# Preparing each GLA chunk one block ahead, with doubled tiles, in a hybrid decoder layer

## What is computed

```
log_a = log_sigmoid(g_lr @ gla_w_gate + gla_b_gate) / 16
b = cumsum(log_a, within a chunk);  b_last = b at the chunk's end
q_dec = q * dk**-0.5 * exp(b);  k_inv = k * exp(-b);  k_end = k * exp(b_last - b)
a_intra = tril(q_dec @ k_inv.T)
o = a_intra @ v + q_dec @ state
state = exp(b_last) * state + k_end.T @ v
o_gla = head_rms_norm(o) * gla_norm_g * silu(g_r)
```

## Time and profile before

| what | value |
|---|---|
| time, median of 2 runs | 3582.77 us (3580.89 to 3584.64) |
| the profiled execution's own time | 3579.59 us |
| its span, core 6 (slowest of 3555.3 to 3577.9) | 3577.9 us |
| mean granted TensorE clock, core 6 | 0.805 |
| busy: PE, DVE, ACT, POOL | 61%, 44%, 43%, 10% |
| HBM over the span | 92 GB/s |

### The profile page before, as it was taken

One profiled execution on the slowest core, in us unless ns is written; L12 is line 12 of the kernel. 1 busy time (PEld: TensorE's weight loads), 2 busy tenths in 40 slices (PEclk: granted clock), 3 DMA queues, 4 the chain that ended last, 5 costly groups with the idle time before them and its releaser, 6 DMA issues.

```text
span 3577.9 us, 45263 instructions; the slowest of 8 cores (3555.3 to 3577.9 us)
## 1 busy us (share of the span) xinstructions
PE 2189.3 (61%) x12880; PEld 1112.3 (31%) x13060; DVE 1556.4 (44%) x3607; ACT 1539.4 (43%) x2278; POOL 357.7 (10%) x292
## 2 busy tenths in 40 slices
PE   4924541565756637677764667777546777775653
PEld 0313321343422224333322423333224333332221
DVE  0033231232443364555235555543465455334782
ACT  0000000062069911587662048877501788875130
POOL 1002113200000000122000002210000112000150
PEclk9856765755879968799887869999767899998787
DMA  9438763303300012111432311124321111333222
GB/s 198 149 118 123 125 130 109 126 1 103 104 1 1 1 70 90 52 50 42 124 112 94 101 36 50 52 71 129 103 78 57 60 42 36 101 107 128 77 70 74
DMA packets 208100, 294.80 MB, mean 82 GB/s; under 512 B 92386, under 2 KB 92531, under 8 KB 207219
## 3 DMA queue, kind: packets, MB, share of 16 engines
q1 hardware_dynamic: 127460, 248.34, 21.8%
q0 software_dynamic: 74064, 26.25, 6.1%
q10 hardware_dynamic: 6336, 17.30, 1.5%
HBM read 293.45 MB, written 34.11 MB: 92 GB/s over the span
## 4 chain that ended last, share of the span: by engine, by line
PE 37%; DMA 22%; DVE 15%; issue 12%; ACT 11%; POOL 2%; DVEq 1%; ACTq 0%; SPq 0%; POOLq 0%
PE PP L246 36%; ACT ARENA L252 10%; DMA ARENA<-wd_s 9%; DVE ARENA L255 5%; DVE ARENA L259 4%; DMA ARENA<-w_down 3%; DMA ARENA<-win_s 2%; DMA ARENA<-w_ada 2%; DVE ARENA L262 2%; DMA wu_s<-w_ff_up 2%; POOL ARENA L259 1%; DMA ARENA<-wout_s 1%; DVE ARENA L266 1%; DMA ARENA<-wg_s 1%; DMA ARENA<-w_out 1%
## 5 line engine op out<-in xcount | busy, mean ns | idle before, releaser
L246 PE MATMUL PP<-ARENA 128*128 128x512 bf16 (+3 forms) x4964 | 1003.0, 350 | 441.5 <-DMA ARENA<-wd_s 109.8
L252 ACT ACTIVATE ARENA<-PP 128x1024 f32<-128x1024 f32 (+3 forms) x1251 | 904.2, 744 | 567.5 <-PE PP L246 445.3
L246 PE MATMUL PP<-ARENA,KT 128*128 128x512 bf16 (+3 forms) x1869 | 609.4, 375 | 378.4 <-ACT ARENA L252 335.2
L252 ACT ACTIVATE ARENA<-ARENA 128x1024 bf16<-128x1024 f32 (+7 forms) x882 | 645.0, 733 | 409.4 <-DVE ARENA L725 147.1
L246 PEld LDWEIGHTS PP<-ARENA 128*128 128x128 bf16 (+2 forms) x5064 | 469.0, 102 | 875.0 <-issue 617.7
L255 DVE TENSOR_SCALAR STAT<-PP 128x4 f32<-128x4 f32 (+3 forms) x512 | 81.2, 159 | 744.8 <-PE PP L246 744.0
L259 POOL TENSOR_TENSOR ARENA<-ARENA 128x512 f32<-128x512 f32 (+1 forms) x198 | 271.9, 1373 | 1249.0 <-PE PP L246 409.5
L246 PEld LDWEIGHTS PP<-ARENA,KT 128*128 128x128 bf16 x1920 | 181.9, 103 | 673.5 <-issue 578.8
L246 PE MATMUL PP<-ARENA,NEGUB 128*128 128x512 bf16 (+3 forms) x947 | 355.9, 376 | 0.9
L252 ACT ACT_TABLE_LOAD x12 | 15.4, 1283 | 761.0 <-PE PP L246 755.7
L266 DVE COPY ARENA<-PP 128x512 f32<-128x512 f32 (+5 forms) x249 | 140.2, 564 | 346.5 <-PE PP L246 308.0
(11 more groups left out here) (65 smaller groups left out, 1269.6 us busy)
## 6 DMA issues: line engine op xcount, KB each, us to landing
ARENA<-wd_s SPq DMA_DIRECT2D x286, 256.0 KB, 2.7
ARENA<-wg_s SPq DMA_DIRECT2D x110, 256.0 KB, 2.6
ARENA<-win_s SPq DMA_DIRECT2D x50, 512.0 KB, 3.9
ARENA<-xw SPq DMA_DIRECT2D x49, 512.0 KB, 6.4
ARENA<-w_ada SPq DMA_DIRECT2D x12, 2048.0 KB, 12.6
ARENA<-wu_s SPq DMA_DIRECT2D x88, 256.0 KB, 2.6
ARENA<-win_s SPq DMA_DIRECT2D x78, 256.0 KB, 3.8
ARENA<-w_down ACTq DMA_DIRECT2D x22, 512.0 KB, 3.7
```

The lines of the kernel that those rows point to most:

```text
L246: return S.op("pe", lambda e: e.matmul(out, lhsT=lhsT, rhs=rhs, start=start, stop=stop), reads, writes)
L252: return S.op("act", lambda e: e.activation(out=out, in_=in_, func=func, bias=bias, scale=scale), reads, writes)
```

## The change

The body of phase B's loop is split into `X(j)`, the prep of block j, and `Y(j)`, all the rest. The calls are X(0), X(1), Y(0), X(2), Y(1), X(3), Y(2), Y(3) in each tile. `QD`, `KI`, `KE` and the decay columns get two buffers each, chosen by j % 2; `EU`, `LL`, `EB`, `ENB`, `ED` and all others keep one. Inside `Y` the state products, the update of `S2` and the cast to `S2B` now stand right behind the products `bo` and ahead of the copies `OC`; before, they stood behind the writes of `ON`. The list `deferred` is still served at the end of each block, now of `Y`.

```diff
--- before.py
+++ after.py
@@ -413,9 +413,9 @@
     EB = cv.take([P, 2, 128], F32)
     ENB = cv.take([P, 2, 128], F32)
     ED = cv.take([P, 256], F32)
-    QD = cv.take([P, 2, 128], BF16)
-    KI = cv.take([P, 2, 128], BF16)
-    KE = cv.take([P, 256], BF16)
+    QDs = [cv.take([P, 2, 128], BF16) for _ in range(2)]
+    KIs = [cv.take([P, 2, 128], BF16) for _ in range(2)]
+    KEs = [cv.take([P, 256], BF16) for _ in range(2)]
     AM = cv.take([P, 2, 2, 128], BF16)
     OC = cv.take([P, 2, 2, 128], F32)
     SQ = cv.take([P, 2, 2, 128], F32)
@@ -510,10 +510,12 @@
                 tm_job(21 + 2 * pi, qblocks, ev)
 
     def phase_B(wt):
-        for j in range(4):
+        def X(j):
             blk = 4 * wt + j
             full = blk >= HALO_BLK
             jc = slice(j * 128, (j + 1) * 128)
+            p = j % 2
+            QD, KI, KE = QDs[p], KIs[p], KEs[p]
             bu, bku = nb()
             mm(bu[:, 0:256], LRA[0:33, jc], WGA[0:33, :], True, True, ["LRA", "WGA"], [bku])
             act(EU, bu[:, 0:256], AF.Exp, [bku], ["EU"], scale=-1.0)
@@ -527,20 +529,27 @@
             if full:
                 act(EB, bb3, AF.Exp, [bkb], ["EB"], bias=float(np.log(0.125)))
             act(ENB, bb3, AF.Exp, [bkb], ["ENB"], scale=-1.0)
-            act(STAT[:, 0:2], bb3[:, :, 127], AF.Exp, [bkb], ["DEC"])
+            act(STAT[:, 2 * p:2 * p + 2], bb3[:, :, 127], AF.Exp, [bkb], [("DEC", p)])
             act(ED, bd[:, 0:256], AF.Exp, [bkd], ["ED"])
-            vtt(KI, GKT[:, :, jc], ENB, ALU.mult, ["GKT", "ENB"], ["KI"])
-            vtt(KE, GK[:, j, :], ED, ALU.mult, [("GK", j), "ED"], ["KE"])
+            vtt(KI, GKT[:, :, jc], ENB, ALU.mult, ["GKT", "ENB"], [("KI", p)])
+            vtt(KE, GK[:, j, :], ED, ALU.mult, [("GK", j), "ED"], [("KE", p)])
+            if full:
+                vtt(QD, GQT[:, :, jc], EB, ALU.mult, ["GQT", "EB"], [("QD", p)])
+
+        def Y(j):
+            blk = 4 * wt + j
+            full = blk >= HALO_BLK
+            p = j % 2
+            QD, KI, KE = QDs[p], KIs[p], KEs[p]
             if full:
                 jq = j if wt >= 4 else 3
-                vtt(QD, GQT[:, :, jc], EB, ALU.mult, ["GQT", "EB"], ["QD"])
                 bas = [nb(), nb()]
                 for h in range(4):
                     g2, par = h // 2, h % 2
                     r0 = par * 64
                     ba, bka = bas[par]
                     mm(ba[:, g2 * 128:(g2 + 1) * 128], KI[r0:r0 + 64, g2, :], QD[r0:r0 + 64, g2, :], True, True,
-                       ["KI", "QD"], [bka])
+                       [("KI", p), ("QD", p)], [bka])
                 for par in range(2):
                     ba, bka = bas[par]
                     vtt(AM[:, par], ba[:, 0:256].rearrange("p (g t) -> p g t", g=2),
@@ -553,7 +562,18 @@
                     mm(bo[:, g2 * 128:(g2 + 1) * 128], AM[:, par, g2, :], GV[:, j, h * 128:(h + 1) * 128], True, False,
                        [("AM", par), ("GV", j)], [bko])
                     mm(bo[:, g2 * 128:(g2 + 1) * 128], QD[r0:r0 + 64, g2, :], S2B[r0:r0 + 64, g2, :], False, True,
-                       ["QD", "S2B"], [bko])
+                       [("QD", p), "S2B"], [bko])
+            bk_, bkk = nb()
+            for h in range(4):
+                g2 = h // 2
+                mm(bk_[:, h * 128:(h + 1) * 128], KE[:, g2 * 128:(g2 + 1) * 128], GV[:, j, h * 128:(h + 1) * 128],
+                   True, True, [("KE", p), ("GV", j)], [bkk])
+            for h in range(4):
+                g2, r0 = h // 2, (h % 2) * 64
+                vstt(S2[r0:r0 + 64, g2, :], S2[r0:r0 + 64, g2, :], STAT[r0:r0 + 64, 2 * p + g2:2 * p + g2 + 1],
+                     bk_[r0:r0 + 64, h * 128:(h + 1) * 128], ALU.mult, ALU.add, ["S2", ("DEC", p), bkk], ["S2"])
+            vcopy(S2B[:], S2[:], ["S2"], ["S2B"])
+            if full:
                 for par in range(2):
                     bo, bko = bos[par]
                     vcopy(OC[:, par], bo[:, 0:256].rearrange("p (g t) -> p g t", g=2), [bko], ["OC"])
@@ -569,19 +589,15 @@
                     vtt(ON[:, jq, 512:1024].rearrange("p (g r t) -> p r g t", g=2, r=2)[:, par], OC[:, par],
                         SR[:, j, :].rearrange("p (g r t) -> p r g t", g=2, r=2)[:, par], ALU.mult,
                         ["OC", ("SR", j)], [("ON", jq, 1)])
-            bk_, bkk = nb()
-            for h in range(4):
-                g2 = h // 2
-                mm(bk_[:, h * 128:(h + 1) * 128], KE[:, g2 * 128:(g2 + 1) * 128], GV[:, j, h * 128:(h + 1) * 128],
-                   True, True, ["KE", ("GV", j)], [bkk])
-            for h in range(4):
-                g2, r0 = h // 2, (h % 2) * 64
-                vstt(S2[r0:r0 + 64, g2, :], S2[r0:r0 + 64, g2, :], STAT[r0:r0 + 64, g2:g2 + 1],
-                     bk_[r0:r0 + 64, h * 128:(h + 1) * 128], ALU.mult, ALU.add, ["S2", "DEC", bkk], ["S2"])
-            vcopy(S2B[:], S2[:], ["S2"], ["S2B"])
             for _ in range(6):
                 if deferred:
                     deferred.pop(0)()
+
+        X(0)
+        for j in range(4):
+            if j + 1 < 4:
+                X(j + 1)
+            Y(j)
 
     def phase_C(wt):
         own = wt >= 4
```

## The result

The changed kernel is slower: its ratio to the kernel before is 1.0101, 95% interval 1.0071 to 1.0131. On the 3582.8 us of before that is +36 us (25 to 47). Every ratio here leaves out the executions in a second, slower state, in which the cores of one die show a clearly lower granted clock; milder cases stay in. The forecast was 3619, +36. The profiled execution took 3624.9 us for a span of 3623.4, which is 45.5 more than the span of before.

The account below looks back on a forecast made before the run. Phase B was taken as one serial chain ordered by the engines' queues, no engine holding half. Terms +28 (tiles 4 to 7), +7 (0 and 1), +1 (2 and 3) sum to +36: 3619 us, range 3598 to 3634.

Parts of the forecast that it names:

- The period: Steady block, tiles 4 to 7: EU (block's start E) to next EU 12.82 us against 10.96, state update before OC costing 2.96.
- The tile: Phase B of each of tiles 4 to 7: 54.2 us against 47.2, so +7.0 each and +28 in all.
- the 3.7: Head of each full tile: the second block's EU comes 3.7 us after the tile's first EU.
- The 1.10: Steady block: AM starts at about E+4.5 instead of E+5.60, E being EU's start; all the change earns there, 1.10 us.
- the wait of DEC: Steady block: decay column DEC waited 0.68 us for the state update; two pairs of columns would free it.
- Tiles 0 and 1: First S2B comes after the second block's prep, +3.5 us, passed through the weight casts to the tile's end; +7 for both.
- Tiles 2 and 3: Net +1 us for both, bounds -3 and +4; tile 3's projections still wait for the memset of QT.
- +3.4 and up to -3.74: Blocks 9 to 11, ScalarE's queue: two preps before the first six folds (+3.4 us), one fewer between groups (up to -3.74).
- The first: Rival, chance 0.06: prep and state update find cover, period 9.86 us, tile 42.4, kernel 3572 us.
- The second: Rival, chance 0.04: tile 3's projections start one group of folds, 47 us, earlier for good; kernel 3572 us.
- The third: Rival, chance 0.07: first block's delay in tiles 0 and 1 doesn't pass, casts held by other transfers; kernel 3612 us.
- The fourth: Rival, chance 0.05: TensorE's products in turn add 2 us in 16 blocks, stretches beside folds worsen; kernel 3650 us.

## Why the prediction was right, point by point

- **The period.** Forecast 12.82, measured 12.79. AM came at E+4.33 (forecast 4.5), OC was pushed back by 5.14 - 2.04 = 3.10 (2.96), the rest 2.91 and 0.41 as forecast. Two small errors, -0.17 and +0.14, cancel, so that the period is right to 0.03 is partly luck.
- **The tile.** Forecast 54.2 against 47.2, +7.0 (the terms as written add up to 54.28); measured 54.7 against 47.0, +7.7. The second block's EU came 4.04, 4.39, 2.42 and 3.24 behind the first, 3.5 in the mean, so the 3.7 was no cause. Three periods took 38.4 to 39.2 instead of 38.5, and the last block from AM to the next EU's place 8.5 in tiles 6 and 7 and 8.8 in tiles 4 and 5 instead of 8.3, the 0.14 of OC and in tiles 4 and 5 a pause of 0.5 on VectorE, of which the rows don't show a cause.
- **Which part costs.** The forecast laid all of the loss on the state update's place. That is shown by the two runs that make one move each: +8.8 a tile for it, +0.8 for prep ahead, +7.7 together.
- **What the change earns.** The 1.10 was near the right size (AM from E+5.60 to E+4.33 is 1.27) and was partly laid to the wrong cause. I named the wait of DEC as a part; the run with two decay columns shows that it is worth nothing. Two things earned: the state update no longer stood in front of KI (E+3.86 before), and AM no longer waits for its scores' turn. The runs with one move each show them apart: AM at E+5.03 with the first alone, at E+5.01 with the second alone, 0.6 each.
- **Tiles 0 and 1.** Forecast +3.5 each. First EU to first S2B went from 5.9 to 10.6 in tile 0 (+4.7) and from 6.3 (402.39 - 396.08) to 9.5 (407.37 - 397.86) in tile 1 (+3.2). It passed to the end of tile 0, as the traces with the old order there show; for tile 1 the marks lie too close to tell.
- **Tiles 2 and 3.** Forecast +1 with -3 to +4. From first S2B of tile 2 to the end of phase B of tile 3, 231.7 became 227.6, and the delay of that first S2B is 9.4 against 6.3: -4.0 + 3.1 = -0.9. The forecast's two terms here, +3.4 and up to -3.74, are borne out: the folds of tile 2 end 138.2 behind S2B of block 8 instead of 142.3. For the same reason the memset stood at 653.74 and not at 656. It held the projections.
- **The sum.** 30.9 + 7.9 - 0.9 = +38 by the stages, +36 by the ratio, +36 forecast. The full tiles cost 3 us more than the 28 forecast and tiles 2 and 3 about 2 less than the +1; that the ratio gives the forecast's very number is luck, as its interval is 25 to 47.

**The rivals.** The first (cover for prep and update) fell in the changed kernel, with the gap on ScalarE longer than before. The Trainium skill ("Perfetto Trace Analysis", Optimization Strategy) has the rule that a repeating gap can mean too few buffers. It says so of the engine that should be saturated, and ScalarE, busy for 43% of the span, need not be that engine. The rule is borne out only in a small part: doubled tiles with prep ahead took the period from 10.96 to 10.36, and the same tiles in another queue order took it to 8.64. The second (tile 3 earlier for good) was held by the memset as forecast; with the memset early it was worth 22 us and not the 47 of a group of folds, since tile 3's first EU stands behind the last fold on ScalarE's queue. The third fell for tile 0: the delay passed. The fourth did not come about: the period is 12.79 and not 2 us more.

## What to carry to other kernels

Where each engine takes its instructions in queued order, "one step ahead" helps only as far as the ahead step stands in the other engines' idle time: place each of its instructions in a gap, do not put the whole step in front. When a piece is moved in such a queue, cost what now stands behind it: here five short VectorE instructions in front of the output chain, and the wait for their product, cost 3.1 us in each of 16 blocks, and prep ahead alone cost nearly nothing. A wait in the trace earns its length only if nothing else of the next step comes as late.

## What was unexpected of the hardware

In the changed kernel the cast of S2B took 1.67 us at 574.22 and 0.92 at 535.50, and 0.29 elsewhere; each of the two began inside a multiplication of GpSimd (573.39 to 575.74, 533.94 to 536.28) and ended 0.15 behind it. In the kernel before the one at 527.43 took 2.07, again beside such a multiplication. All eleven traces together have ten casts that began inside one; they took 0.92 to 2.21 and each ended 0.14 to 0.16 behind it. A cast that began before the multiplication, as the one at 608.05 before (multiplication from 608.30), kept its 0.29. The Trainium skill ("SBUF — State Buffer", SBUF: two separate sides) says that VectorE in some modes and GpSimd share a port pair as an exclusive lock, and the loser waits for the whole instruction; the rows agree with it. Other VectorE work that the two traces show beside these multiplications, such as the updates of S2 (1.70), kept its time; all of it reads PSUM. It cost nothing here, as VectorE waits for ScalarE or for the memset soon after; beside a busier VectorE the folds might cost something, which no run tries.
